# A third weight chunk split ahead in six normed stages, and a lagging second tile in three stages begun by a pair

## The reference

```python
h = rmsnorm(x) * gain + shift          # x: 1024 features x 512 tokens
a = w_up.T @ h                         # 44 tiles of 128 rows, 8 slices of 128 deep
x = x + gate * (w_dn.T @ mid(a))       # 8 tiles, then the next norm
```

## Time and profile before

| | |
|---|---|
| time, median of 3 runs | 3460.77 us (3457.66 to 3462.41) |
| profiled execution, its own time | 3468.48 us |
| its span | 3466.8 us |
| PE busy | 3355.3 us, 97% |
| DVE busy | 2003.4 us, 58% |
| ACT busy | 1110.9 us, 32% |
| mean granted clock of TensorE | 0.985 |

### The profile page before, as it was taken

The page is one execution under the profiler, slowest core; times in us unless marked ns, Lnnn a source line. Parts: engine busy times, 40 slices in busy tenths (PEclk is TensorE's granted clock), DMA queues, the critical chain, the costliest instruction groups (busy, mean ns, idle before and its releaser), DMA issues. The chain is left out here.

```text
span 3466.8 us, 38774 instructions
## 1 busy us (share of the span) xinstructions
PE 3355.3 (97%) x13840; PEld 2517.3 (73%) x13840; DVE 2003.4 (58%) x2815; ACT 1110.9 (32%) x1503; POOL 134.1 (4%) x230
## 2 busy tenths in 40 slices
PE   6999899999899999998999999999999999999999
PEld 3446678887678888666788864578887757888887
DVE  6685666535658864555666359766644454455523
ACT  2223422224632222443433210343323343242222
POOL 1000000000001000000000040000000100000000
PEclk9999999999999999999999999999999999999999
DMA  7222355542125543212222311122233222222222
GB/s 285 81 68 81 121 180 191 178 132 73 49 73 194 194 155 94 74 48 74 85 96 95 95 64 51 47 85 97 95 96 132 77 76 70 97 96 87 97 97 85
DMA packets 100426, 361.20 MB, mean 104 GB/s; under 512 B 11152, under 2 KB 11168, under 8 KB 100064
## 3 DMA queue, kind: packets, MB, share of 16 engines
q1 hardware_dynamic: 79088, 280.34, 24.4%
q0 software_dynamic: 20080, 75.27, 6.4%
q10 hardware_dynamic: 1152, 4.19, 0.3%
HBM read 357.66 MB, written 2.10 MB: 104 GB/s over the span
## 5 line engine op out<-in xcount | busy, mean ns | idle before, releaser
L2327 DVE TENSOR_TENSOR weight_lo<-weight_ring,weight_hi 128x1024 fp32r<-128x1024 f32 (+1 forms) x464 | 560.2, 1208 | 914.3 <-ACT weight_hi L1613 908.0
L1613 ACT ACTIVATE weight_hi<-weight_ring 128x1024 fp32r<-128x1024 f32 (+1 forms) x464 | 484.9, 1046 | 1609.4 <-PE proj_banks L889 999.4
L889 PE MATMUL proj_banks<-h_lo,weight_hi 128*128 128x512 f32 x1704 | 665.0, 390 | 0.0
L889 PE MATMUL proj_banks<-h_hi,weight_hi 128*128 128x512 f32 x1344 | 523.2, 389 | 4.1 <-DVE weight_lo L2327 4.1
L889 PE MATMUL proj_banks<-h_hi,weight_lo 128*128 128x512 f32 x1344 | 522.9, 389 | 0.0
L889 PEld LDWEIGHTS proj_banks<-h_lo,weight_hi 128*128 128x128 f32 x1704 | 320.9, 188 | 67.0
L889 PEld LDWEIGHTS proj_banks<-h_hi,weight_hi 128*128 128x128 f32 x1344 | 252.3, 188 | 57.4 <-issue 5.7
L889 PEld LDWEIGHTS proj_banks<-h_hi,weight_lo 128*128 128x128 f32 x1344 | 252.3, 188 | 52.5
L889 PE MATMUL proj_banks<-mid_hi,weight_hi 128*128 128x512 f32 x704 | 273.9, 389 | 0.0
L889 PE MATMUL proj_banks<-mid_lo,weight_hi 128*128 128x512 f32 x704 | 273.9, 389 | 0.0
L889 PE MATMUL proj_banks<-mid_hi,weight_lo 128*128 128x512 f32 x704 | 273.9, 389 | 0.0
(11 more groups left out here) (416 smaller groups left out, 5160.2 us busy)
## 6 DMA issues: line engine op xcount, KB each, us to landing
weight_ring<-in_w_up SPq DMA_DIRECT2D x176, 512.0 KB, 3.3
ada_ring<-in_ada POOLq DMA_DIRECT2D x96, 512.0 KB, 3.8
weight_ring<-in_w_dn SPq DMA_DIRECT2D x64, 512.0 KB, 3.6
weight_ring<-in_w_br SPq DMA_DIRECT2D x32, 512.0 KB, 3.2
weight_ring<-in_w_upr SPq DMA_DIRECT2D x32, 512.0 KB, 3.2
weight_ring<-in_w_dnr SPq DMA_DIRECT2D x32, 512.0 KB, 3.2
weight_ring<-in_w_dn SPq DMA_DIRECT2D x32, 384.0 KB, 3.1
cond<-in_ada POOLq DMA_DIRECT2D x20, 512.0 KB, 4.4
```

Of the source, the lines that this page charges most:

```text
L889: last = mm(proj.banks[:, u % RING, :], stationary(split0 + n)[:, w], moving(k), start=k + m == 0, stop=k == kt - 1 and m == 2)
L1613: return nc.scalar.activation(out, in_, func, **kw)
L2327: return v.tensor_tensor(out, a, b, op)
```

## The change

- Six normed stages (`THIRD`): chunk 2 of the stage gets a home of its own in a free part of `mid_hi` and `mid_lo`. ACT rounds it (`round_third`) and DVE takes its rest (`rest_third`) at the end of the stage before, ahead of the last residual tile. In the stages after `dn0` and `dn1`, ACT waits for the first piece of the last `dn` tile to be used, since PE still reads there.
- `first_pair` becomes `first_three`. After the 32 matmuls it takes four rest products of tile 0, the `hi` and `lo` products of slices 0 to 3 of tile 2 (8 matmuls), the other four of tile 0, the eight of tile 1, slices 4 to 7 of tile 2 (8 matmuls), and the eight rest products of tile 2. The stage goes on with tile 3.
- The rounding and rest of chunk 2 leave their old place behind tile 0; that of chunk 3 stays behind tile 1. The first four tiles of the `up` loops on ACT and DVE stand outside the loop for this. Chunk 1 counts two in `w_rounded` and `w_split`.
- In `abo`, `cdo` and `mout` the second tile lags: by three slices in `abo` (2, 3, 7) and `cdo` (3, 6, 7), by four slices throughout `mout`. `cout` stays as it is.
- In `sq` the statistics of tiles 0 and 1 now follow one another after the three tiles, and then comes tile 3.

```diff
-    def first_pair(name, r, lo):
-
-        split0 = c.first_split[name]
+    def first_three(name, r, lo):
+
+        split0, third = c.first_split[name], list(THIRD).index(r)
...
-        for t in range(2):
-            for k in range(KD):
+
+        def low(t, ks):
+            for k in ks:
                 pe.wait_ge(s["h_ready"], h_count(r, k))
                 last = mm(proj.bank((name, t)), c.hi(split0 + t)[:, k * P:(k + 1) * P], lo(k), start=False, stop=k == KD - 1)
...
+        def third_high(ks):
+            for k in ks:
+                bank = open_bank(proj, (name, 2)) if k == 0 else proj.bank((name, 2))
+                if k == 0:
+                    pe.wait_ge(s["third_split"], third + 1)
+                for weight in (c.hi, c.lo):
+                    mm(bank, weight(split0 + 2)[:, k * P:(k + 1) * P], c.norm_hi(r, k), start=k == 0 and weight == c.hi, stop=False)
+
+        low(0, range(4))
+        third_high(range(4))
+        low(0, range(4, KD))
+        low(1, range(KD))
+        third_high(range(4, KD))
+        low(2, range(KD))
...
-    for k in (6, 1, 2, 3, 7):
+    for k in (6, 1):
         out_step(k)
+    for t in range(2):
+        for k in (2, 3, 7):
+            out_step(k, (t,))
...
     norm(2)
-    first_pair("sq", 2, c.H_lo)
+    first_three("sq", 2, c.H_lo)
     for t in range(1, 9):
-        if 2 <= t < 8:
+        if 3 <= t < 8:
             split_feature_tile("sq" if t < 4 else "sk", t % 4, c.H_hi, c.H_lo)
...
-    for k in (2, 3, 6, 7):
-        pe.wait_ge(*mix.emptied(("pool", k) if k < 4 else ("sb", k - 4)))
-        pair_step("cdo", k, c.cdo_hi, c.cdo_lo)
+    pe.wait_ge(*mix.emptied(("pool", 2)))
+    pair_step("cdo", 2, c.cdo_hi, c.cdo_lo)
+    for t in range(2):
+        for k in (3, 6, 7):
+            if t == 0:
+                pe.wait_ge(*mix.emptied(("pool", k) if k < 4 else ("sb", k - 4)))
+            part_step("cdo", t, k, c.cdo_hi, c.cdo_lo)
...
-    for k in range(KD):
-        pe.wait_ge(s["m_lo_ready"], k + 1)
-        pair_step("mout", k, c.mout_hi, c.H_lo)
+    for k in range(KD + 4):
+        if k < KD:
+            pe.wait_ge(s["m_lo_ready"], k + 1)
+            part_step("mout", 0, k, c.mout_hi, c.H_lo)
+        if k >= 4:
+            part_step("mout", 1, k - 4, c.mout_hi, c.H_lo)
...
+    def round_third(r):
+
+        name = SPLIT_UP[r]
+        if NORM_AFTER[r] in ("dn0", "dn1"):
+            act.wait_ge(*split_use(c, c.first_split[NORM_AFTER[r]] + 3 * (KD - 1)))
+        chunk = c.first_chunk[name] + 2
+        act.wait_ge(*c.chunk_landed(chunk))
+        st.done(f(c.hi(c.first_split[name] + 2), c.slot(chunk), ACT.Copy), s["third_rounded"])
...
             if k == KD - 1:
+                round_third(NORM_OF[name])
                 prepare(NORM_OF[name])
...
+THIRD = {1: (16, 20), 2: (0, 2), 3: (16, 20), 4: (6, 0), 5: (14, 20), 7: (20, 20)}
...
+    def rest_third(r):
+
+        split, chunk = c.first_split[SPLIT_UP[r]] + 2, c.first_chunk[SPLIT_UP[r]] + 2
+        dve.wait_ge(s["third_rounded"], list(THIRD).index(r) + 1)
+        st.done(tt(c.lo(split), c.slot(chunk), c.hi(split).bitcast(F32), ALU.subtract), s["third_split"])
...
     for t in range(8):
-        rest_s(t + SPLIT_RING)
+        if t > 0:
+            rest_s(t + SPLIT_RING)
         if t >= 4:
```

More of the change, by code:

```diff
@@ L402, in __init__ @@
                 m += splits_of(s)
+        self.third = {self.first_split[SPLIT_UP[r]] + 2: at for r, at in THIRD.items()}
     def T(self, i, n=1):
@@ L876, in four_tiles @@
         def four_tiles(i, first=0):
+            home = split0 + (4 * len(per) if first == 0 else 0)
             for j in range(first, 4):
@@ L896, in split_loop @@
         if norm is not None:
-            first_pair(name, norm, lo)
-            started = True
+            first_three(name, norm, lo)
+            four_tiles(0, first=3)
         if started:
             four_tiles(0, first=2)
-        with pe.Fori(1 if started else 0, tiles // 4) as i:
+        with pe.Fori(1 if started or norm is not None else 0, tiles // 4) as i:
             four_tiles(i)
@@ L1169, in tensor_program, with out_step @@
     gate_half(0, 0)
-    def out_step(k):
-        if k < 4:
+    def out_step(k, tiles=(0, 1)):
+        if tiles[0] == 0 and k < 4:
             pe.wait_ge(s["gla_lo"], k + 1)
-        else:
+        elif tiles[0] == 0:
             pe.wait_ge(*mix.emptied(("av", NB - 1, k - 4)))
-        pair_step("abo", k, c.abo_hi, c.abo_lo, first=4)
+        for t in tiles:
+            part_step("abo", t, k, c.abo_hi, c.abo_lo, first=4)
     units = [(b, h) for b in range(NB) for h in range(4)]
@@ L1307, in tensor_program @@
     m_lo = lambda k: c.norm_lo(4, k)
-    first_pair("mqk", 4, m_lo)
-    for t in range(2, 8):
+    first_three("mqk", 4, m_lo)
+    for t in range(3, 8):
         split_feature_tile("mqk", t, c.H_hi, m_lo)
@@ L1637, in round_chunk, with st_round @@
         w = chunk_floats(name, n)
-        st_round(f(c.hi(split)[:, 0:w], c.slot(chunk)[:, 0:w], ACT.Copy))
-    def st_round(ins):
-        ins.then_inc(s["w_rounded"], 1)
+        st_round(f(c.hi(split)[:, 0:w], c.slot(chunk)[:, 0:w], ACT.Copy), 2 if split + 1 in c.third else 1)
+    def st_round(ins, chunks=1):
+        ins.then_inc(s["w_rounded"], chunks)
+    def round_third(r):
[5 more added lines that the diff above has]
+        st.done(f(c.hi(c.first_split[name] + 2), c.slot(chunk), ACT.Copy), s["third_rounded"])
     def round_ahead(name, i, j):
@@ L1646, in round_ahead @@
         act.wait_ge(c.landed[chunk % RING], i * 16 + 16 * (chunk // RING + 1))
-        st_round(f(c.hi(split), c.slot(chunk), ACT.Copy))
+        st_round(f(c.hi(split + RING), c.slot(chunk), ACT.Copy))
     def round_down(layer):
@@ L1855, in swiglu, with four @@
         u0 = proj.number[(up, 0)]
-        with act.Fori(0, 2 * FT // 4) as i:
+        def four(i, first=0):
             for j in range(4):
@@ L1859, in swiglu @@
                 act.wait_ge(proj.full_sem, i * 4 + u + 1)
-                round_ahead(up, i, j)
+                if j >= first:
+                    round_ahead(up, i, j)
                 if j % 2 == 0:
@@ L1864, in swiglu @@
                     f(T(52 + p), proj.banks[:, u % RING, :], ACT.Silu).then_inc(proj.empty_sem[u % RING], 1)
+        four(0, first=1)
+        with act.Fori(1, 2 * FT // 4) as i:
+            four(i)
         round_down(layer)
@@ L2023, in conv_ffn @@
                     act.wait_ge(proj.full_sem, i * 4 + u + 1)
-                    round_ahead(up, i, 2 * p + g)
+                    if 2 * p + g >= first:
+                        round_ahead(up, i, 2 * p + g)
                     if g == 0:
@@ L2427, in rest_ahead @@
         dve.wait_ge(s["w_rounded"], i * 4 + (split + 1))
-        tt(c.lo(split), c.slot(chunk), c.hi(split).bitcast(F32), ALU.subtract).then_inc(s["w_split"], 1)
+        tt(c.lo(split + RING), c.slot(chunk), c.hi(split + RING).bitcast(F32), ALU.subtract).then_inc(s["w_split"], 1)
     def split_mid(i, layer, p, raw):
@@ L2447, in residual @@
                 sum_up(r, k - 1)
+            if k == KD - 1 and r in THIRD:
+                rest_third(r)
             dve.wait_ge(*proj.filled(key))
@@ L2690, in swiglu, with four @@
         u0 = proj.number[(up, 0)]
-        with dve.Fori(0, 2 * FT // 4) as i:
+        def four(i, first=0):
             for j in range(4):
@@ L2694, in swiglu @@
                 ada_in_loop(i, j, layer, ctx)
-                rest_ahead(up, i, j)
+                if j >= first:
+                    rest_ahead(up, i, j)
                 if j % 2 == 1:
@@ L2703, in swiglu @@
             ada_columns(i, layer, ctx)
+        four(0, first=1)
+        with dve.Fori(1, 2 * FT // 4) as i:
+            four(i)
     def last_row(layer, ctx, j):
```

45 lines of the change are left out of this document (30 added, 15 removed).

## The result

| | before | after |
|---|---|---|
| median of 4 runs | 3461.59 us | 3439.62 us |
| lowest and highest | 3457.66, 3464.44 | 3436.98, 3442.91 |
| profiled execution, its own time | 3468.48 us | 3436.98 us |
| its span, mean granted clock | 3466.8 us, 0.985 | 3435.1 us, 0.989 |

The ratio is 0.9931, with a 95% interval from 0.9919 to 0.9944: some 22 us faster (19 to 28 by the interval), against a forecast of 3439 us.

What follows compares the result with a forecast made beforehand. PE, busy 97% of the span, was taken as the bound. Terms 2.9 + 8.5 + 2.7 - 2.1 + 7.0 = 19.0 us from waits plus 2.5 from the clock gave 3460.8 - 21.5 = 3439 us, range 3431 to 3450.

Steps and rivals of the forecast that it cites:

- The fill in `up0`, `mqk`, `up2`, `up3`: At these stages' starts, tile 2's matmuls fill PE's waits for rests: 2.9 us won in up0, 8.5 in the others.
- The thinnest cover: In mqk DVE's convolution taps precede chunk 3's rest, which ends near L+8.3, before PE asks at L+9.07.
- `up1`: Gain 3.1 us at tile 3, 2.7 after tile 4, with waits of about 0.7 and 0.2 left there.
- `sq`: Loss of 2.1 us, bounds 0 and -3.2: chunk 3's rest waits behind DVE's first reciprocal and scaling, half clock follows.
- The pairs: Lagging second tiles shorten PE's stalls: 1.36 us in abo, 1.35 in cdo, 4.28 in mout, together 7.0.
- The clock: Half clock behind the stalls in abo, cdo and mout goes: 0 to 5 us, 2.5 taken for the medians.
- the 19.0 from waits: Sum of PE's shortened waits over the six normed stages and the pairs, sq's loss included: 19.0 us.
- The clock gives nothing back: Half-clock stretches move to other stalls and sq pays the full 3.2 us: 18 us won, 3443 us; chance 0.18.
- Tile 3 late everywhere: DVE or ACT reaches chunk 3 late in the other five stages, their gain falling from 14.1 to 3: 3451 us; chance 0.08.
- Slower: Chunk 2's load lands late and ACT, in order, holds up everything in the norm: 3469 us; chance 0.04.
- Not measurable: The fills only move waits to later tiles on an unseen bound: 3458 us; chance 0.04.

Runs made afterwards that it cites:

- Experiment 2: The changed kernel with the pairs in abo, cdo and mout put back as before, the third chunk ahead kept in all six stages; 3447.2 us, ratio 0.9961.
- experiment 4: The changed kernel with DVE taking chunk 3's rest in sq ahead of the first reciprocal, the other rests unmoved; 3440.84 us, ratio 0.9939.
- experiment 3: The changed kernel with sq alone put back to two tiles, the other five stages keeping three; 3438.63 us, ratio 0.9932.
- experiment 7: The changed kernel with the added rounding on ACT and rest on DVE each done twice in all six stages; 3440.51 us, ratio 0.9927.
- experiment 5: The changed kernel; in sq DVE takes rests of chunks 3 to 6 one step earlier, ACT rounds chunks 4 and 5 before its head wait; 3430.37 us, ratio 0.9899.
- experiment 9: The changed kernel with chunk 3's rest in the up stages taken ahead of tile 1's modulation rows on DVE; 3441.55 us, ratio 0.9933.
- experiment 8: The changed kernel with cout's second tile also lagging by four slices; 3440.47 us, ratio 0.9928.
- experiment 6: The changed kernel with seven unneeded 128x512 matmuls put in front of tile 3 of sq, filling PE's wait; 3438.54 us, ratio 0.9926.

## Why the prediction was right

**The fill in `up0`, `mqk`, `up2`, `up3`**: forecast 2.9 and 8.5; tile 3 came at 9.47, 9.16, 9.17 and 9.19 us, where 9.38 and 9.07 were forecast, without a wait. Experiment 2 shows the same with the pairs as before. The thinnest cover, `mqk`'s convolution taps ahead of chunk 3's rest, held: that rest was done 0.76 us before PE asked for it, where 0.8 was forecast.

**`up1`**: forecast 2.7, measured 3.2, in a stretch without half clock in either execution. The wait at tile 3 was there (0.62, forecast 0.7), that at tile 4 (0.2) was not.

**`sq`**: forecast -2.1. The mechanism was right in each step (root, reciprocal at 811.67, scaling, rest, tile 3 at 16.94 us where 16.77 was forecast, half clock behind it) and is shown by experiment 4. The Trainium skill (TensorE: Matmul & The Clock Gate, the section Architectural detail: the array is 16× 32×32, not 1× 128×128) has VectorE's queue strictly first in, first out; the runs agree, since the same subtraction, whose rounding ACT had ended by 807.5, ran at 815.85 behind the reciprocal and at 807.55 when the program put it ahead (experiment 4). From the stage's first matmul tile 7 came 1.8 later than before. Against a two-tile `sq` whose clock did not fall, experiment 3, it is 3.1, near the lower bound of -3.2.

**The pairs**: forecast 1.36, 1.35 and 4.28. 2.05 fell to 0.69 in `abo` and `cdo`, `mout` lost both its waits. Experiment 2 bears out `mout` with 4.4 us.

**The clock**: this is the term that was mis-sized. It was taken as 0 to 5 us, from the three pairs alone. In the profiled executions about 12 came back (31.7 less the 19.0 from waits and 0.6 at the start; the record of the clock allows at most 12.0). Of the 24.0 us at half clock that went, the three pairs have only 10.2; `cout` and places between `sq` and `cdo` that the change does not touch have the rest. So for the execution like the profiled one the forecast was 24.0 us of gain, and 31.5 were measured (3468.48 - 3436.98).

For the medians 2.5 was taken, and 22.0 - 19.0 = 3.0 was measured, but that agreement is partly luck. With the interval of 19 to 28 us, the clock's share in the medians can be anything from 0 to 9. The four executions of after form two groups, 3436.98 and 3437.01 at a mean clock of 0.989, and 3442.24 and 3442.91 at 0.986; the median of 3439.62 is the middle of the gap, and no execution took that time. The executions of before in the experiments spread too: near 3461.5 us at 0.987, near 3466.5 at 0.986 and from 3467 to 3470.5 at 0.984 or 0.985. Against the 3442.6 of after at 0.986, those of before at 0.987 are 18.9 higher and those at 0.986 are 23.9 higher. That fits the 19.0 of the waits without proving it, since one step in the last digit of the clock goes with 2 to 5 us.

**The rivals.** *The clock gives nothing back* (3443) is close to two of the four runs of after (3442.24 and 3442.91); the median lies 3.4 below it, and the profiled execution did get clock back. *Tile 3 late everywhere* is out by the four stages above. *Slower*, through work ahead of the norm, is out by the norms themselves, which take as long as before (experiment 7); what a late load would do was not tried. *Not measurable* is out by the ratio.

## What to carry to other kernels

More tiles contracted together at a stage's start pay only if the next tile's preparation does not stand behind the work that waits for these tiles: look at each engine's program for what is queued ahead of the next operand, and move the ready step ahead of the waiting one, at every tile and not at the first alone (experiments 4 and 5). Moving a step forward pays only if its own input is there by then (experiment 9), and a lag pays only where inputs come faster than one tile uses them (experiment 8). The best version here is experiment 5, some 9 us under the changed kernel; the intervals of their ratios, 0.9884 to 0.9913 and 0.9919 to 0.9944, do not meet.

## What the runs showed of the hardware

- Which idle time is followed by 1.2 GHz is not told by its length. `mout` as it was before has two stalls, 2.09 at its start and 2.05 before tile 2. Windows of the 3.7 us behind each, kernel before and then experiment 2, where both stalls are the same (1.94 and 1.89 by the trace's brackets in both): the low clock has changed places.

```profile
1606.70:1610.40 3.70, 3.70 (x16) 3.06 (x17) 2.50 (x4) 1.27 (x2) 0.16 (x1) 1.00 0.44 142
1619.10:1622.80 3.70, 3.70 (x11) 2.92 (x12) 2.23 (x3) 0.71 (x2) 0.00 (x0) 0.63 0.68 215
```

```profile
1591.50:1595.20 3.70, 3.69 (x9) 2.92 (x10) 2.54 (x4) 1.26 (x2) 0.12 (x1) 0.54 0.40 142
1605.50:1609.20 3.70, 3.70 (x16) 3.06 (x17) 2.27 (x3) 0.76 (x2) 0.00 (x0) 1.00 0.65 194
```

  The stall of `cout`, not changed at all, was followed by clock 0.59 over 3.7 us before and by 1.00 after. The stalls of 5.2 and 5.6 in `sq` were followed by half clock, and not when PE was kept busy (experiment 6).
- Whether shortened waits elsewhere moved these drops, or only chance did, no run tells: they also differ between executions where the programs do not. Up to the pair of `abo` the changed kernel and experiment 5 are the same, and their traces show 41.0 and 51.2 us at half clock there.
- Two executions of one program can differ by 5 to 6 us, the longer one at the lower mean clock. A difference of a few us between kernels is better read from a stage, from its first matmul to a given tile, than from the whole: from `up0` to `sq`, where no trace has half clock, every kernel with three tiles took 367.20 to 367.24 us.
- DVE's reciprocal of 128x512 float32 takes 3.35 us, more than four times the 0.69 to 0.75 of its additions and scalings of such a tile, and is what makes the order in `sq` matter.
